# Bias rows stored from 128 partitions in eight parts, and the third FFN's first two units alternated with halves of the compression

## The chip, the cores and the metric

The kernel runs on one core of one Trainium2 chip. The metric is the device time of one execution, in microseconds. A profile is one execution of the program, taken by the hardware profiler; times in it count from the start of its span. The engines are TensorE (PE, with its weight loads as PEld), VectorE (DVE), ScalarE (ACT), GpSimd (POOL) and SyncE (SP), which issues most of the DMAs.

## What is computed

Two transformer blocks run one after the other on x of 1 x 256 x 1024, float32. The first has three attention branches and an MLP of width 4096. The second has four SwiGLU FFNs of width 2816 (FFN 0 to 3 in the kernel), a gated spatial mixer between FFN 0 and 1, and an attention with compressed, selected and window keys between FFN 2 and 3. Two pieces of the second block matter here:

```
def swiglu(x, w1, w3, w2):
    return (jax.nn.silu(x @ w1) * (x @ w3)) @ w2

def compress(kv, pe, w1, b1, w2):      # once for keys, once for values
    ...
    blocks = blocks + pe[None, None, :, None, :]
    flat = blocks.transpose(0, 1, 3, 2, 4).reshape(B, n_cmp, G, CMP_LEN * Dh)   # 15 blocks, 2048 wide
    return jax.nn.gelu(flat @ w1 + b1, approximate=False) @ w2                  # w1: 2048 x 256

    def head_bias(dist):               # rel_table: 32 buckets x 16 heads
        return rel_table[rel_bucket(dist)].reshape(dist.shape + (G, HG)).transpose(2, 3, 0, 1)
```

The bias of a head depends on the distance alone, so one row of 383 numbers for each of the 16 heads holds all of it. The third FFN and the compression are independent of each other: the compression reads what the second FFN left, and is used only in the attention behind the third.

## The kernel before

**Units and the ring.** Every weight comes in units of 128 x 2048 float32 (1 MiB). The order of the units is the list that `plan_units` returns. SyncE loads them in that order into a ring of three slots; a load waits until the unit three places earlier has been split, or, for the compression's units ("cw", i), which aren't split, until TensorE has used it (the semaphore `unit_used`, raised by the first matmul behind a unit: `settle`). Splitting means two float32r halves: ScalarE copies the unit, which rounds it (L1438), VectorE subtracts (L1858), and the two go into one of three split slots; the last unit of a stage goes into the tensor `two`. For ten-odd units GpSimd subtracts in place of VectorE (L2460); ("w3", 0, 0) is one of them. A product of float32 numbers is then three matmuls.

**The stages' order** is written out by hand for each engine, and each engine goes through its own list in order. `plan_tiles` gives every TensorE output a PSUM bank: banks 0 to 3 in turn for tiles, banks 4 to 7 for the accumulators of the down products, which `clear_acc` zeroes before a stage and which the norm behind the stage reads.

**The MLP** has 16 chunks of 256 hidden columns. A chunk is 48 matmuls of the up unit, relu on ScalarE (L1610), square and split on VectorE (L2193, L2174, L2176; the last one raises `hid_ready`), and 48 matmuls of the down unit, done one chunk later. `down_last` at the end does half of the last but one down unit, then alternates with the last, so that the norm can start by halves of rows. The first matmuls of the next FFN follow as soon as the rows' transposes are there.

**The bias rows.** While the MLP's first chunks run, TensorE makes the 16 rows with one matmul (`rel_rows`, 33 x 16, against `onehot`, 33 x 383), VectorE copies them out (L2220), and GpSimd stores each head's row 128 times into the DRAM tensor `rel_scratch`, one DMA for each head (L2504), paced by `hid_ready`. Head h waits for h + 1 hidden chunks, 14 at most. Behind the stores in GpSimd's queue come ("w3", 0, 0), the gain rows and the mixer's constants. The scratch is read back once, skewed, for the attention late in the kernel.

**The third FFN** (f = 2) starts, without a norm of its own, behind the keys' and values' units. TensorE does the keys' compression (two units, 64 columns a matmul, straight from the ring), the unit ("w1", 2, 0), the values' compression, ("w3", 2, 0), the clears, and then chunk by chunk. ScalarE does four gelus of the compression (L1762), rounds ("w3", 2, 0), then ("w1", 2, 1), and goes on with the silus. The values' compression writes to the banks that the keys' compression had.

Of the kernel before, what the change touches and what calls it, by code (L numbers as in the profile page):

```python
# [81 lines left out]
def plan_units():  # L82
# [21 lines left out]
    u += third[0:1] + [("cw", i) for i in range(2, 4)] + third[1:]  # L104
# [30 lines left out]
def plan_tiles():  # L135
# [42 lines left out]
    names += [("ch", s, m) for s in range(2) for m in range(2)]  # L178
    names += ffn(2) + half_norm(7, 0) + [("ck",), ("cv",)] + half_norm(7, 1)
    names += [("qg",)] + [("q", i) for i in range(8)] + [("qt",)]  # L180
    names += mix(MIX2) + norm(8) + ffn(3) + norm(9)
    held, out, turn = [0] * 4, {}, 0
    for seq, name in enumerate(names):
        if name[0] == "m":
            bank = name[1] % MLP_BODY
        elif name[0:2] == ("n", 2):
            bank = 2 + name[3]
        elif name[0] == "hm":
            bank = 3 - name[1]
        elif name[0] == "rel":  # L190
            bank = 3
        elif name[0:2] == ("ch", 1):
            bank = out[("ch", 0, name[2])][0]
        else:
            bank, turn = turn % 4, turn + 1
# [65 lines left out]
WO_EARLY = 2  # L261

# [33 lines left out]
def two_blocks(nc, t, out):  # L296
    ctx = ExitStack()
    with ctx:
# [95 lines left out]
        rel_out = take(at, N_REL)[0:NH]  # L394
# [58 lines left out]
        tile_read = [sem(f"tile_read{i}") for i in range(4)]  # L453
# [7 lines left out]
        rel_out_ready, rel_stored, rel_back = sem("rel_out_ready"), sem("rel_stored"), sem("rel_back")  # L461
# [123 lines left out]
        def _(sp):  # L585
# [135 lines left out]
        def _(pe):  # L721
# [338 lines left out]
            def mlp(n):  # L1060
# [79 lines left out]
            def ffn(f, between=None):  # L1140
# [11 lines left out]
                def first_by_features():  # L1152
# [33 lines left out]
                clear_acc()  # L1186
                done = MLP_CHUNKS + f * FFN_CHUNKS + (8 if f else 0)

                def chunk(c):
# [7 lines left out]
                    up_w3(tiles, parts(("w3", f, c + 1), KT))  # L1197
                    have(("w2", f, c))
# [112 lines left out]
            def compress(s):  # L1311
                tiles = [open_tile(("ch", s, m)) for m in range(2)]
                pe.wait_ge(cx_ready, s + 1)
                for h in range(2):
                    have(("cw", 2 * s + h))
                    for m in range(2):
                        for j in range(8):
                            ins = mm(tiles[m][:, 0:HD], up_unit(("cw", 2 * s + h))[:, j, m * P:(m + 1) * P],
                                     cx[:, s, 8 * h + j].rearrange("p g i -> p (g i)"), h == 0 and j == 0,
                                     h == 1 and j == 7)  # L1320
                            if j == 0:
                                settle(ins)
                        if h:
                            ins.then_inc(tile_done, 1)
                    owed[0] += 1

            compress(0)
            ffn(2, lambda: compress(1))
# [84 lines left out]
        def _(act):  # L1413
# [234 lines left out]
            def ffn(f, following):  # L1648
# [110 lines left out]
            for s in range(2):  # L1759
                for m in range(2):  # L1760
# [61 lines left out]
        def _(dve):  # L1822
# [355 lines left out]
            def mlp():  # L2178
# [34 lines left out]
                by_tokens(0)  # L2213
                low_hidden(0)
# [5 lines left out]
                dve.tensor_copy(rel_out, o[0:NH, 0:N_REL]).then_inc(frees(("rel",)), 1)  # L2220
# [231 lines left out]
        def _(pool):  # L2452
# [56 lines left out]
            pool.wait_ge(rel_stored, 16 * NH)  # L2509
# [75 lines left out]
```

## Time and profile before

| | us |
| --- | --- |
| median of 3 runs | 1580.91 |
| lowest and highest | 1579.22, 1581.44 |
| the profiled execution | 1582.14 |
| its span | 1580.4 |
| TensorE busy in the span | 1507.0 (95%) |
| VectorE busy | 932.0 (59%) |
| ScalarE busy | 658.6 (42%) |
| GpSimd busy | 105.2 (7%) |
| share of TensorE in the chain that ended last | 83% |

The page lists, for the whole span, the busy time of each engine, the chain of work that ended last and the costliest groups of instructions. A matmul's busy time overlaps with the next one's. Behind an instruction in a timeline stands, in brackets, how long its engine was idle before it and what ended that. The mean granted clock of TensorE over the span is 0.97 of full speed.

### The profile page before, as it was taken

What the parts mean: (1) busy time and instruction counts of PE and PEld (TensorE: products, weight loads), DVE (VectorE), ACT (ScalarE), POOL (GpSimd) and SP (SyncE); (2) the same over time, 40 slices, a digit from 0 to 9 for tenths busy, and PEclk for the clock granted to TensorE, in tenths of its full rate; (3) what the DMA queues carried; (4) which work ended last, traced back from release to release, by engine and by line L of the source; (5) the groups of instructions that cost most, each with busy time, mean ns of one, the idle gap of its engine ahead of it and who ended that gap; (6) DMA issues with size and microseconds to landing.
All of it is one profiled execution on the core that took longest, in us unless ns stands there. A gap on an engine that the chain in (4) does not pass through costs nothing.

```text
span 1580.4 us, 25559 instructions
## 1 busy us (share of the span) xinstructions
PE 1507.0 (95%) x10597; PEld 1372.9 (87%) x10608; DVE 932.0 (59%) x1370; ACT 658.6 (42%) x831; POOL 105.2 (7%) x85
## 2 busy tenths in 40 slices
PE   8989999999789999999999999989999999999997
PEld 6978977898679999998889998989999876799997
DVE  5886367565475556657775556635555464365556
ACT  5655433343234334453343334333333455343332
POOL 0012141000020000100010001000001120100000
PEclk9999999999989999999999999999999988999999
DMA  7533445999956556564456555575555510355651
GB/s 251 159 111 105 159 163 138 192 217 208 162 193 230 190 191 211 172 187 160 141 194 194 185 190 191 168 237 190 192 188 177 187 54 1 107 167 189 190 191 64
DMA packets 191639, 268.45 MB, mean 170 GB/s; under 512 B 5852, under 2 KB 164736, under 8 KB 191294
## 3 DMA queue, kind: packets, MB, share of 16 engines
q1 hardware_dynamic: 186336, 250.05, 48.1%
q0 software_dynamic: 4336, 15.91, 7.9%
q10 hardware_dynamic: 878, 1.21, 0.3%
q8 instruction: 66, 1.08, 0.3%
q14 instruction: 23, 0.19, 0.0%
HBM read 261.92 MB, written 4.19 MB: 168 GB/s over the span
## 4 chain that ended last, share of the span: by engine, by line
PE 83%; DVE 8%; DMA 3%; ACT 3%; issue 1%; POOL 0%; SPq 0%; DVEq 0%; ACTq 0%
PE bank L725 81%; PE bank L748 2%; DVE split L1858 2%; ACT split L1438 2%; DMA ring<-in_ffn_w 1%; DMA ring<-in_w_mlp_out 1%; DVE resid L1935 1%; DVE resid L1943 1%; DVE stats L1914 1%; DVE resid L1912 1%; DMA ring<-in_w_in 1%; ACT act_out L1460 0%; DVE hid_hi L2174 0%; DVE arena L2055 0%; ACT gain_rows L1564 0%
## 5 line engine op out<-in xcount | busy, mean ns | idle before, releaser
L725 PE MATMUL bank<-hT_hi,split 128*128 128x256 f32 (+1 forms) x3984 | 717.5, 281 | 10.9 <-ACT act_out L1576 5.4
L1858 DVE TENSOR_TENSOR split<-ring,split 128x2048 fp32r<-128x2048 f32 x210 | 479.6, 2285 | 388.7 <-ACT split L1438 383.5
L725 PEld LDWEIGHTS bank<-hT_hi,split 128*128 128x128 f32 (+1 forms) x3984 | 616.2, 189 | 18.1 <-issue 8.9
L1438 ACT ACTIVATE split<-ring 128x2048 fp32r<-128x2048 f32 (+1 forms) x224 | 426.8, 1907 | 365.2 <-PE bank L725 327.3
L725 PE MATMUL bank<-hT_lo,split 128*128 128x256 f32 (+1 forms) x1992 | 558.4, 280 | 0.0
L725 PEld LDWEIGHTS bank<-hT_lo,split 128*128 128x128 f32 (+1 forms) x1992 | 376.3, 189 | 2.4
L725 PE MATMUL bank<-split,hid_hi 128*128 128x512 f32 x992 | 288.8, 397 | 0.3 <-DVE split L1858 0.2
L725 PEld LDWEIGHTS bank<-split,hid_hi 128*128 128x128 f32 x992 | 182.9, 189 | 41.2 <-issue 1.2
L725 PE MATMUL bank<-split,hT_hi 128*128 128x256 f32 (+1 forms) x896 | 179.0, 298 | 6.7 <-DVE split L1858 4.4
L725 PE MATMUL bank<-split,hid_lo 128*128 128x512 f32 x496 | 160.0, 396 | 0.0
L725 PEld LDWEIGHTS bank<-split,hT_hi 128*128 128x128 f32 x896 | 143.9, 190 | 15.2 <-DVE split L1858 5.1
L2460 POOL TENSOR_TENSOR split<-ring,split 128x2048 fp32r<-128x2048 f32 x14 | 64.2, 4583 | 1034.5 <-ACT split L1438 866.1
L725 PE MATMUL bank<-split,hT_lo 128*128 128x256 f32 (+1 forms) x448 | 129.9, 296 | 0.0
L1610 ACT ACTIVATE act_out<-bank 128x256 f32<-128x256 f32 (+1 forms) x104 | 43.2, 417 | 179.1 <-PE bank L725 179.0
L725 PEld LDWEIGHTS bank<-split,hid_lo 128*128 128x128 f32 x496 | 93.5, 188 | 22.3
L725 PEld LDWEIGHTS bank<-split,hT_lo 128*128 128x128 f32 x448 | 85.3, 190 | 2.4
L725 PE MATMUL bank<-arena 64*128 64x256 f32 (+6 forms) x442 | 70.8, 322 | 12.6 <-DVE row_max L2072 4.5
L725 PEld LDWEIGHTS bank<-arena 64*128 64x128 f32 (+4 forms) x442 | 51.7, 179 | 29.8 <-issue 12.8
L2176 DVE TENSOR_TENSOR hid_lo<-hid,hid_hi 128x256 fp32r<-128x256 f32 (+1 forms) x112 | 51.4, 459 | 4.0 <-DVE hid_hi L2174 0.2
L2271 DVE SCALAR_TENSOR_TENSOR hid<-act_out,bank 128x256 f32<-128x256 f32 x82 | 34.3, 418 | 30.6 <-ACT act_out L1610 30.6
L725 PE MATMUL bank<-two,hid_hi 128*128 128x512 f32 x96 | 34.9, 416 | 18.1 <-DVE hid_lo L2176 18.1
L2174 DVE CAST hid_hi<-hid 128x256 fp32r<-128x256 f32 (+1 forms) x112 | 39.0, 348 | 3.8
(202 smaller groups left out, 994.0 us busy)
## 6 DMA issues: line engine op xcount, KB each, us to landing
ring<-in_ffn_w SPq DMA_DIRECT2D x132, 1024.0 KB, 5.3
ring<-in_w_in SPq DMA_DIRECT2D x19, 1024.0 KB, 5.2
ring<-in_w_mlp_in SPq DMA_DIRECT2D x16, 1024.0 KB, 9.3
ring<-in_w_mlp_out SPq DMA_DIRECT2D x16, 1024.0 KB, 7.9
ring<-in_sgu_w_in SPq DMA_DIRECT2D x16, 1024.0 KB, 5.5
ring<-in_sgu_w_out SPq DMA_DIRECT2D x8, 1024.0 KB, 4.9
ring<-in_kv_w SPq DMA_DIRECT2D x6, 1024.0 KB, 5.4
ring<-in_w_out SPq DMA_DIRECT2D x4, 1024.0 KB, 5.0
```

The lines of the kernel that those rows point to most:

```text
L725: ins = pe.matmul(o, lhsT, rhs, start=start, stop=stop)
L748: return pe.transpose(o, a, ident[0:n, 0:n])
L1438: act.activation(halves(q, n)[0], ring[:, u % SLOTS, 0:n], ACT.Copy).then_inc(hi_ready, 1)
L1610: act.activation(act_out[:, b, 0:cols], banks[b][:, 0:cols], func).then_inc(act_ready, 1)
L1858: dve.tensor_tensor(lo, ring[:, u % SLOTS, 0:n], hi.bitcast(F32), ALU.subtract).then_inc(split_ready, 1)
L1912: link(dve.scalar_tensor_tensor(out=r, in0=r, scalar=ALPHA if n >= 4 else 1.0, in1=acc[2 * b + h][:, :], op0=ALU.mult, op1=ALU.add))
L1914: link(dve.bn_stats(stats[:, b, h, :], r))
L1935: link(dve.scalar_tensor_tensor(out=d, in0=r, scalar=mv[:, b, 0:1], in1=gain_bc[:, cols], op0=ALU.subtract, op1=ALU.mult))
L2174: dve.tensor_copy(hi, raw).then_inc(hid_rounded, 1)
L2176: return dve.tensor_tensor(lo, raw, hi.bitcast(F32), ALU.subtract)
L2271: dve.scalar_tensor_tensor(out=raw, in0=act_out[:, b, 0:S], scalar=0.5, in1=banks[b][:, S:2 * S], op0=ALU.mult, op1=ALU.mult).then_inc(til ...
L2460: pool.tensor_tensor(split_lo[:, place, :], ring[:, u % SLOTS, :], split_hi[:, place, :].bitcast(F32), ALU.subtract).then_inc(split_ready, 1)
```

## The change

The bias rows: `rel_rows` is copied to `rel_wide`, where each head's column stands eight times, so that the matmul gives 128 rows. Each partition then stores its row 16 times, in eight DMAs of two copies from all 128 partitions. Part j waits for j + 3 hidden chunks.

The third FFN: the order of the units becomes ("w1", 2, 0), ("cw", 2), ("w3", 2, 0), ("cw", 3), ("w1", 2, 1) and so on, and TensorE does the values' compression in two halves, one behind each of the first two units. Its output goes to banks 5 and 6, two accumulators, and the clears move behind the second pair of units and behind ScalarE's gelus. ScalarE rounds ("w3", 2, 0) right behind the keys' gelus and does the values' gelus behind the first two silus.

```diff
@@ plan_units
-    u += third[0:1] + [("cw", i) for i in range(2, 4)] + third[1:]
+    u += third[0:1] + [("cw", 2)] + third[1:2] + [("cw", 3)] + third[2:]
@@ plan_tiles
-    names += [("ch", s, m) for s in range(2) for m in range(2)]
-    names += ffn(2) + half_norm(7, 0) + [("ck",), ("cv",)] + half_norm(7, 1)
+    third = ffn(2)
+    names += [("ch", 0, m) for m in range(2)] + third[0:2] + [("ch", 1, m) for m in range(2)] + third[2:]
+    names += half_norm(7, 0) + [("ck",), ("cv",)] + half_norm(7, 1)
...
-            bank = out[("ch", 0, name[2])][0]
+            bank = 5 + name[2]
@@ SyncE, ffn
                 if f == 2:
                     load(("cw", 2))
+                load(("w3", f, 0))
+                if f == 2:
                     load(("cw", 3))
-                load(("w3", f, 0))
@@ TensorE, mlp
                 pe.wait_ge(rel_in, 32)
-                pe.wait_ge(fills, 2)
+                pe.wait_ge(rel_wide_ready, 1)
                 o = open_tile(("rel",))
-                ins = mm(o[0:NH, 0:N_REL], rel_rows, onehot, True, True)
+                ins = mm(o[:, 0:N_REL], rel_wide, onehot, True, True)
@@ TensorE, ffn
-                    between()
+                    between(0)
                     have(("w3", f, 0))
                     up_w3(tiles, parts(("w3", f, 0), KT))
+                    between(1)
...
-                clear_acc()
+                if f in TOK:
+                    clear_acc()
...
+                    if c == 0 and f not in TOK:
+                        for m in range(2):
+                            tile_copied(pe, ("ch", 1, m))
+                        clear_acc()
@@ TensorE, the compression
-            compress(0)
-            ffn(2, lambda: compress(1))
+            pe.wait_ge(cx_ready, 1)
+            compress(0, 0)
+            compress(0, 1)
+
+            def second_compression(h):
+                pe.wait_ge(cx_ready, 2)
+                compress(1, h)
+
+            ffn(2, second_compression)
@@ ScalarE, ffn
                     silu(0, 0)
                     silu(0, 1)
+                    between()
                     rounds(0)
@@ ScalarE, the third FFN
+            compressed(0)
             round_unit(("w3", 2, 0))
-            ffn(2, (("qg", 0), ("q", 0)))
+            ffn(2, (("qg", 0), ("q", 0)), lambda: compressed(1))
@@ VectorE, mlp
                 by_tokens(0)
+                dve.wait_ge(rel_in, 32)
+                dve.wait_ge(fills, 2)
+                dve.tensor_copy(rel_wide.rearrange("p (h r) -> p h r", h=NH),
+                                rel_rows.unsqueeze(2).to_broadcast([33, NH, P // NH])).then_inc(rel_wide_ready, 1)
                 low_hidden(0)
...
-                dve.tensor_copy(rel_out, o[0:NH, 0:N_REL]).then_inc(frees(("rel",)), 1)
+                dve.tensor_copy(rel_out, o[:, 0:N_REL]).then_inc(frees(("rel",)), 1)
@@ GpSimd
-            for h in range(NH):
-                pool.wait_ge(hid_ready, min(h + 1, MLP_CHUNKS - 2))
-                pool.dma_start(rel_dram.ap()[h:h + 1], rel_out[h:h + 1, :].unsqueeze(1).to_broadcast([1, P, N_REL])
-                               ).then_inc(rel_stored, 16)
+            copies = NH // REL_PARTS
+            rows = rel_dram.ap().rearrange("h (r i) n -> (h r) i n", r=P // NH)
+            for j in range(REL_PARTS):
+                pool.wait_ge(hid_ready, j + 3)
+                pool.dma_start(rows[:, j * copies:(j + 1) * copies, :],
+                               rel_out.unsqueeze(1).to_broadcast([P, copies, N_REL])).then_inc(rel_stored, 16)
```

`REL_PARTS` is 8, and the two later waits on `rel_stored` ask for 16 * REL_PARTS in place of 16 * NH.

## Rows read from the trace of the kernel before

**Rows 1.** The list of waits of TensorE: engine, line, waited for; us in total, times, longest.

```profile
PE bank L725 <- DVE hid_lo L2176: 18.3, 2, 18.1
```

**Rows 2.** The timeline of TensorE at the MLP's end: start, us, what.

```profile
409.36 0.27 PE L725 MATMUL bank<-hT_hi,split 128*128 128x256 f32 x1
...
420.56 0.27 PE L725 MATMUL bank<-hT_hi,split 128*128 128x256 f32 x1
...
423.24 0.40 PE L725 MATMUL bank<-split,hid_hi 128*128 128x512 f32 x1
441.76 0.77 PE L725 MATMUL bank<-two,hid_hi 128*128 128x512 f32 x1 [18.13 <-DVE hid_lo L2176]
...
453.31 0.36 PE L725 MATMUL bank<-split,hT_hi 128*128 128x256 f32 x1
```

**Rows 3.** The timelines of the other engines and SP's queue in that stretch.

```profile
401.35 1.55 POOL L2504 DMA_DIRECT2D rel_scratch<-arena  x3 [10.68 <-DVE hid_lo L2176]
...
403.28 0.38 SPq L642 DMA_DIRECT2D ring<-in_w_mlp_out  x1
...
427.33 1.91 ACT L1438 ACTIVATE two<-ring 128x2048 fp32r<-128x2048 f32 x1 [15.25 <-DMA ring<-in_w_mlp_out]
...
411.10 0.43 DVE L2174 CAST hid_hi<-hid 128x512 fp32r<-128x512 f32 x1
411.56 0.69 DVE L2176 TENSOR_TENSOR hid_lo<-hid,hid_hi 128x512 fp32r<-128x512 f32 x1
...
436.24 4.65 DVE L2174 CAST hid_hi<-hid 128x512 fp32r<-128x512 f32 x1
```

**Rows 4.** The DMA issues of the whole run: KB each, median us to landing.

```profile
rel_scratch<-arena POOLq DMA_DIRECT2D x16, 191.5 KB, 9.3
...
out<-resid SPq DMA_DIRECT2D x4, 256.0 KB, 2.0
```

**Rows 5.** The timeline of TensorE at the first FFN's end.

```profile
633.05 0.39 PE L725 MATMUL bank<-two,hid_hi 128*128 128x512 f32 x1
...
643.27 0.36 PE L725 MATMUL bank<-split,hT_hi 128*128 128x256 f32 x1
```

**Rows 6.** The DMA queues between 255 and 445 us: packets, MB, share.

```profile
q1 hardware_dynamic: 21749, 33.54, 49.6%
q0 software_dynamic: 1034, 3.16, 45.4%
```

**Rows 7.** The timeline of TensorE at the third FFN's start.

```profile
1027.83 0.36 PE L725 MATMUL bank<-hT_hi,split 128*128 128x256 f32 x1
...
1033.52 7.25 PE L725 MATMUL bank<-arena,ring 128*128 128x64 f32 x64
...
1045.30 0.58 PE L725 MATMUL bank<-hT_hi,split 128*128 128x256 f32 x1 [4.53 <-DVE split L1858]
...
1053.85 0.47 PE L725 MATMUL bank<-hT_hi,split 128*128 128x256 f32 x1
```

**Rows 8.** The timeline of ScalarE in that stretch.

```profile
1026.31 1.28 ACT L1762 ACT_TABLE_LOAD   x1 [4.96 <-PE bank L725]
1027.61 0.76 ACT L1762 ACTIVATE arena<-bank,colv 128x60 f32<-128x60 f32 x2
...
1041.02 1.90 ACT L1438 ACTIVATE split<-ring 128x2048 fp32r<-128x2048 f32 x1
```

**Rows 9.** SP's queue there, and the second of its two compression loads (1025 to 1028.3).

```profile
1024.70 3.89 SPq L642 DMA_DIRECT2D ring<-in_cmp_w  x2
...
ring<-in_cmp_w SPq DMA_DIRECT2D x1, 1024.0 KB, 5.8
```

**Rows 10.** Three stretches: from:to, length, busy of each engine, granted clock, DMA share, GB/s.

```profile
268.00:269.00 1.00, 0.17 (x2) 0.14 (x2) 0.79 (x2) 1.00 (x1) 0.00 (x0) 1.00 0.89 273
1272.00:1273.00 1.00, 0.24 (x2) 0.00 (x0) 1.00 (x4) 0.15 (x1) 0.55 (x1) 1.00 0.15 57
1275.00:1276.00 1.00, 1.00 (x6) 0.86 (x5) 0.90 (x6) 0.52 (x3) 0.00 (x0) 0.63 1.09 386
```

More of the change, by code:

```diff
@@ L177, in plan_tiles @@
     names += [("kT", s, f) for s in (0, 1, 2, 4) for f in range(2)]
-    names += [("ch", s, m) for s in range(2) for m in range(2)]
-    names += ffn(2) + half_norm(7, 0) + [("ck",), ("cv",)] + half_norm(7, 1)
+    third = ffn(2)
+    names += [("ch", 0, m) for m in range(2)] + third[0:2] + [("ch", 1, m) for m in range(2)] + third[2:]
+    names += half_norm(7, 0) + [("ck",), ("cv",)] + half_norm(7, 1)
     names += [("qg",)] + [("q", i) for i in range(8)] + [("qt",)]
     names += mix(MIX2) + norm(8) + ffn(3) + norm(9)
-    held, out, turn = [0] * 4, {}, 0
+    held, out, turn = [0] * 8, {}, 0
     for seq, name in enumerate(names):
@@ L261 @@
 WO_EARLY = 2
+REL_PARTS = 8
 def rounded_before(f):
@@ L393, in two_blocks @@
         onehot = take(at, N_REL)[0:33]
-        rel_out = take(at, N_REL)[0:NH]
+        rel_out = take(at, N_REL)
+        rel_wide = take(at, P)[0:33]
         at = [2 * KT * S]
@@ L452, in two_blocks @@
         tile_done = sem("tile_done")
-        tile_read = [sem(f"tile_read{i}") for i in range(4)]
+        tile_read = [sem(f"tile_read{i}") for i in range(7)]
         x_in = [sem(f"x_in{b}") for b in range(NB)]
@@ L460, in two_blocks @@
         cw2_in = sem("cw2_in")
-        rel_out_ready, rel_stored, rel_back = sem("rel_out_ready"), sem("rel_stored"), sem("rel_back")
+        rel_wide_ready, rel_stored, rel_back = sem("rel_wide_ready"), sem("rel_stored"), sem("rel_back")
         cols_ready = sem("cols_ready")
@@ L1309, in _, with compress @@
                 owed[0] += 1
[L1311 to L1325, printed above, removed]
-            compress(0)
-            ffn(2, lambda: compress(1))
+            def compress(s, h):
+                tiles = [bank_of(("ch", s, m)) if h else open_tile(("ch", s, m)) for m in range(2)]
+                have(("cw", 2 * s + h))
+                for m in range(2):
+                    for j in range(8):
+                        ins = mm(tiles[m][:, 0:HD], up_unit(("cw", 2 * s + h))[:, j, m * P:(m + 1) * P],
+                                 cx[:, s, 8 * h + j].rearrange("p g i -> p (g i)"), h == 0 and j == 0,
+                                 h == 1 and j == 7)
+                        if j == 0:
+                            settle(ins)
+                    if h:
+                        ins.then_inc(tile_done, 1)
+                owed[0] += 1
+            pe.wait_ge(cx_ready, 1)
[5 more added lines that the diff above has]
+            ffn(2, second_compression)
             pe.wait_ge(cw2_in, 32)
@@ L1646, in mlp, with ffn @@
                 round_unit(("w3", 0, 0))
-            def ffn(f, following):
+            def ffn(f, following, between=None):
                 first = ("w1", f, 1)
@@ L1758, in _, with compressed @@
             act.wait_ge(fills, 4)
-            for s in range(2):
+            def compressed(s):
                 for m in range(2):
@@ L2501, in _ @@
             tile_copied(pool, ("rel",))
-            for h in range(NH):
-                pool.wait_ge(hid_ready, min(h + 1, MLP_CHUNKS - 2))
-                pool.dma_start(rel_dram.ap()[h:h + 1], rel_out[h:h + 1, :].unsqueeze(1).to_broadcast([1, P, N_REL])
-                               ).then_inc(rel_stored, 16)
+            copies = NH // REL_PARTS
[4 more added lines that the diff above has]
+                               rel_out.unsqueeze(1).to_broadcast([P, copies, N_REL])).then_inc(rel_stored, 16)
             low_unit(("w3", 0, 0))
             load_rows(4)
-            pool.wait_ge(rel_stored, 16 * NH)
+            pool.wait_ge(rel_stored, 16 * REL_PARTS)
             pool.dma_start(ws, t["sgu_w_s_2"][0].rearrange("g p s -> p g s")).then_inc(sgu_in, 16)
@@ L2531, in _ @@
             pool.memset(pc, 0.0).then_inc(fills, 1)
-            pool.wait_ge(rel_stored, 16 * NH)
+            pool.wait_ge(rel_stored, 16 * REL_PARTS)
             pool.dma_start(rel, bass.AP(rel_dram, P - 1, [[N_REL - 1, P], [P * N_REL, NH], [1, S]])).then_inc(rel_back, 16)
```

## The prediction

> **What bounds the kernel now.** I read the list of what TensorE waited for first. One entry stands out, a single wait of 18.1 us that ended with VectorE's low half of a hidden chunk [rows 1]. TensorE is busy nearly everywhere else, so the time is its own work plus a few holes, and a change pays only by what it takes out of a hole or adds to one. Then I read TensorE's timeline on both sides of that hole, and the other engines' in the same stretch. The last block of the MLP opens with twelve products of the old chunk (ending about 423.5) and stops; it goes on at 441.76 and reaches the first product of the next FFN at 453.31 [rows 2]. VectorE is the name in the wait, but not the cause. ScalarE rounded the last down unit at 427.33, as soon as it had landed, and everything in its queue came behind it. That unit was issued at 403.28, 24.05 us earlier, and 2 us ahead of it GpSimd had issued the last three row stores [rows 3]. VectorE's cast then sat 4.65 us at 436.24, where it takes 0.43 us in the loop, because GpSimd's own subtraction of ("w3", 0, 0) ran at the same time [rows 3]. So three things in a row: stores, then a late load, then a collision. The second hole is in the third FFN: 4.53 us ahead of its first w3 unit, after which the matmuls run at half the clock for a while [rows 7].
>
> **Why the stores hurt.** A store of 191.5 KB takes 9.3 us to land, about 21 GB/s; a store of 256 KB from 128 partitions takes 2.0 us, 128 GB/s, at the end of the kernel [rows 4]. Between 255 and 445 us the GpSimd queue moved 3.16 MB in 45.4% of the sixteen engines' time, the weights 33.54 MB in 49.6% [rows 6]: nearly nine times as much time for each byte. What differs is that each old store reads one partition (one head's row, repeated 128 times).
>
> **Part 1, the stores.** The same 3.1 MB now go out in 8 parts of 383 KB, from 128 partitions (each head's row on eight). Added: one VectorE copy of 33 x 128 after the first by_tokens, a bias matmul that makes 128 rows where it made 16 with the same 383 columns, and a copy of 128 x 383 where it was 16 x 383. The last two have the length of their free size, so nothing; the first is bounded by 0 and about half a microsecond (the cast of 128 x 512 in the loop is 0.43) and falls where VectorE waits for TensorE and ScalarE anyway, so I take 0. The wait on rel_wide_ready stands ahead of a matmul that comes a whole down block later. GpSimd's stores now wait for hidden chunks 3 to 10 instead of 1 to 14; behind them in its queue are only ("w3", 0, 0) and the gain rows, both needed after 415 us. A chunk takes 11.20 us (409.36 to 420.56, rows 2), so the last part, four chunks ahead of the stores of 401.35, goes out at about 356.5, some 47 us before the load that was late. No row shows a GpSimd store from 128 partitions. From below its price is the 2.0 us of the output store scaled by size, 3 us; from above it is the old time for each byte, 5.4 us of all sixteen engines for an old store, so 10.8 for a part. I take the former, since partitions are the only thing that changed. The Trainium skill (SBUF — State Buffer, "Door 1: the DMA port swizzle") gives 27.6 GB/s for partitions 0 to 3 and 328 for all 128, both for 1 MiB; the old stores' 21 GB/s agrees, and by it a part would take some 3 us as well.
>
> Now what is late next. The load of 403.28 lands by 410 (5.8 us without such stores beside it, rows 9) and the next three follow as slots come free. In the loop the low half of a hidden chunk ends at 412.25, 2.6 us after the last up product of its chunk (409.36 and 0.27); one chunk of 11.20 later that is 423.45 [rows 2, 3]. TensorE's twelve products of cover end at 423.47, so it starts the last unit at about 423.7: a hole of 0.3 us instead of 18.1. The collision goes too: ScalarE rounds ("w3", 0, 0) only after the last relu, so GpSimd starts near 423.3, after the cast. From the first product of the last unit to the first of the next FFN the same code takes 10.22 us at full clock in the first FFN (633.05 to 643.27) and took 11.55 here [rows 2, 5]. So 453.31 becomes 423.7 + 10.2 = 433.9, a gain of 19.4 us; the RMS norm here has shorter VectorE steps than the layer norm of the twin, worth up to 0.6 more. I take **19.5 us**.
>
> **Part 2, the third FFN.** Before, from 1033.52: the second compression 7.25 us, the hole 4.53 us (ScalarE in its order does both gelus of that compression before it rounds w3, at 1041.02), then w3 and the clears until 1053.85, 8.55 us, where a unit at full clock takes 5.7 (1027.83 to 1033.52) and the clears some 0.7 [rows 7, 8]. So 4.5 + 2.2 = 6.7 us can be had.
>
> After, in order. A half of the compression is 3.6 us. The w3 load takes the place of ("cw", 3), the second issue in the row of 1024.70, at 1028.2, and lands as that one did after 5.8 us, at 1034.0 [rows 9]. From ScalarE's rounding to TensorE's first product is 4.28 us (1041.02 to 1045.30, rows 7, 8): w3 can start at 1038.3, where TensorE is free at 1033.5 + 3.6 = 1037.1, a hole of 1.2. ("w1", 2, 1) now takes the ring slot of ("cw", 2), which is freed by the first product behind it, at 1038.7; it lands at 1044.5 and can be used at 1048.8. TensorE is free at 1038.3 + 5.7 + 3.6 = 1047.6: a hole of 1.2 again. ScalarE goes on from 1046.5 with a table load, two silus, another table load and two gelus (1.28 + 0.8 + 1.28 + 0.8, rows 8) and rounds ("w3", 2, 1) at 1050.6, usable at 1054.9; TensorE wants it at 1048.8 + 5.7 = 1054.5: 0.4. The moved clears cost what they did. Behind the new wait of ScalarE for the second compression are three roundings, of which only that one is near. The sum: 6.7 - 1.2 - 1.2 - 0.4 = **3.9 us**. The new banks 5 and 6 remove a wait that was already met, so nothing.
>
> **Does a hole of 1.2 us cost clock?** A wait of 0.83 us at 268 left the granted clock at 1.00; one of 1.05 us in 1272 to 1273, in a stretch of small matmuls, was followed by 0.63 in 1275 to 1276 [rows 10]. The stretch here is dense like that of 268, so I take no fall; one fall would cost the 2.2 us above.
>
> **Sum.** 19.5 + 3.9 = 23.4 us. The profiled execution took 1582.14 us with a span of 1580.4, the median of the three runs is 1580.91; the difference of 1.2 us is kept out, and the gain is taken from the median: 1557.5 us (1558.7 against the profiled execution).
>
> **Rivals.**
> (a) Part 2 gives little or nothing. Its holes cost clock once or twice (2.2 each), or the loads come a microsecond later. For it: three new waits within 20 us; against it: TensorE is dense between them. Time 1580.9 - 19.5 less 2 or 0 = 1559.4 to 1561.4.
> (a2) A switch of ScalarE's tables costs twice its load. The change puts two switches ahead of the third rounding; at 1.28 us more for each, the third hole is 3.0 us instead of 0.4 and the clock falls behind it (2.2), so part 2 comes out at 3.9 - 2.6 - 2.2 = -0.9 and the time at 1562.3. Against it: the load of 1026.31 takes 1.28 us and the gelu stands right behind it at 1027.61 [rows 8]. The Trainium skill (ScalarE: Activation LUTs, "What ACT_TABLE_LOAD costs") has it this way, with a drain of about 1.38 us beside each load.
> (b) The collision stays. If ("w1", 0, 0), issued at about 408.4, lands later than some 417, VectorE is late for the last cast and meets GpSimd: 4.6 us and a fall of clock of 2.2, so 1564. Loads without such stores beside them land in 5.8, so this needs 3 us more.
> (c) Slower. The time of a store is a price for each byte, not for reading one partition. Then a part holds the sixteen engines 10.8 us, two weight units 5.9 (94 us for 33.54 MB, rows 6), together 16.7 us in a chunk of 11.20: eight chunks would each be 5.5 us longer, 44 us, against 23 gained: 1602. It begins to hurt where a part costs over 5.3 us, and eats the gain from 8.2. Against it: the 2.0 us of the output store.
> (d) The change doesn't do what it says: another late load keeps the hole near 18 us, and only part 2 shows: 1577.
>
> **How the numbers follow.** Forecast 0.74, (a) 0.11, (a2) 0.03, (b) 0.05, (c) 0.05, (d) 0.02. The low end is part 2 without any hole and the 0.6 of the norm: 1580.9 - 20.1 - 6.7 = 1554.1, taken as 1553.5 for the offset of single runs; the high end takes in (a) and (a2), 1562.5. Left out are (b), (c), (d). This kernel can be told from no change at about 0.2% (3 us). Forecast, (a), (a2) and (b) are faster by more, 0.93, and half of (d) with them, 0.94; same is the other half, 0.01; slower is (c), 0.05.
>
> **What would show it.** Part 1: the 18.1 us wait gone from TensorE's list, stores landing in about 3 us, weight units in the MLP landing near 6, the cast back at 0.43, next FFN 19 to 20 us earlier. Part 2: three waits of about 1 us instead of 4.5, granted clock 1.00 throughout, two more table loads. I am wrong if the stores take over 5 us each, or if the new waits are longer than 2 us and the clock falls.

## The result, and the profile after

The changed kernel takes 1557.13 us (median of 4 runs, 1551.82 to 1560.56), against 1580.98 for the kernel before on the same chip (4 runs, 1579.22 to 1581.44): a ratio of 0.985, with an interval of 0.981 to 0.988. That is 23.9 us less; forecast were 23.4. The profiled execution took 1553.93 us, with a span of 1552.2 and a granted clock of 0.98.

**Part 1.** First the list of what TensorE waited for: engine, line, waited for; us in total, times, longest.

```profile
PE bank L729 <- ACT act_out L1591: 8.9, 3, 3.9
PE bank L729 <- DVE split L1877: 5.4, 4, 3.7
...
PE bank L752 <- DMA shared_rows<-in_cmp_pe: 4.4, 1, 4.4
```

The entry of 18.1 us [rows 1] is gone, and the longest that are left are waits of 4.4, 3.9 and 3.7 us elsewhere. TensorE's timeline at the MLP's end (start, us, what) answers to [rows 2]:

```profile
419.57 0.27 PE L729 MATMUL bank<-hT_hi,split 128*128 128x256 f32 x1
...
422.25 0.40 PE L729 MATMUL bank<-split,hid_hi 128*128 128x512 f32 x1
422.60 0.47 PE L729 MATMUL bank<-two,hid_hi 128*128 128x512 f32 x1
...
432.30 0.35 PE L729 MATMUL bank<-split,hT_hi 128*128 128x256 f32 x1
```

The last unit, the one in `two`, now follows the twelve products of cover without a wait. The next FFN starts at 432.30, where it was 453.31. The MLP's last chunk was 0.99 us earlier anyway (419.57 against 420.56), so 20.0 us are gained here. The timelines of the other engines and of SP's queue in that stretch, as [rows 3]:

```profile
355.49 0.72 POOL L2529 DMA_DIRECT2D rel_scratch<-arena  x1 [10.48 <-DVE hid_lo L2195]
422.38 4.63 POOL L2483 TENSOR_TENSOR split<-ring,split 128x2048 fp32r<-128x2048 f32 x1 [66.17 <-ACT split L1453]
...
402.29 0.38 SPq L645 DMA_DIRECT2D ring<-in_w_mlp_out  x1
...
410.98 1.91 ACT L1453 ACTIVATE two<-ring 128x2048 fp32r<-128x2048 f32 x1
...
421.30 0.43 DVE L2193 CAST hid_hi<-hid 128x512 fp32r<-128x512 f32 x1
```

All three links of the old chain are broken. The last store goes out at 355.49. The load of 402.29 is rounded at 410.98 with no wait for a DMA in brackets, so it landed in less than 8.7 us, where it took 24. The cast takes 0.43 us and ends before GpSimd's subtraction starts at 422.38. In the kernel before the two ran side by side: this is GpSimd's row there, beside the cast of 4.65 us at 436.24 [rows 3].

```profile
436.12 4.49 POOL L2460 TENSOR_TENSOR split<-ring,split 128x2048 fp32r<-128x2048 f32 x1 [33.22 <-ACT split L1438]
```

The DMA queues between 255 and 445 us (packets, MB, share of the sixteen engines' time) and three of the groups of issues there (KB each, median us to landing) answer to [rows 4] and [rows 6]:

```profile
q1 hardware_dynamic: 21760, 33.56, 56.8%
q0 software_dynamic: 1349, 4.89, 7.7%
...
ring<-in_w_mlp_out SPq DMA_DIRECT2D x14, 1024.0 KB, 5.0
ring<-in_w_mlp_in SPq DMA_DIRECT2D x13, 1024.0 KB, 6.0
...
rel_scratch<-arena POOLq DMA_DIRECT2D x8, 383.0 KB, 6.0
```

GpSimd's queue moved half as much again as in [rows 6] (gain rows and the mixer's constants fall into the stretch now) and took 7.7% of the engines' time where it took 45.4%.

**Part 2.** TensorE's timeline at the start of the third FFN, as [rows 7]:

```profile
1006.57 0.36 PE L729 MATMUL bank<-hT_hi,split 128*128 128x256 f32 x1
...
1012.26 3.68 PE L729 MATMUL bank<-arena,ring 128*128 128x64 f32 x32
1016.48 0.39 PE L729 MATMUL bank<-hT_hi,split 128*128 128x256 f32 x1 [0.54 <-DVE split L1877]
...
1022.19 3.68 PE L729 MATMUL bank<-arena,ring 128*128 128x64 f32 x32
1026.31 0.38 PE L729 MATMUL bank<-hT_hi,split 128*128 128x256 f32 x1 [0.44 <-DVE split L1877]
```

One wait of 4.53 us has become two of 0.54 and 0.44, with a half of the values' compression ahead of each. The granted clock is 1.00 in every stretch of 10 us from 1005 to 1045.

**The run stage by stage.** A stage is taken from the first residual add of one norm to that of the next, by VectorE's timeline (before: 235.28, 444.70, 634.64, 787.33, 977.42, 1220.94, 1376.17, 1565.3 us; after: 234.61, 424.27, 613.66, 766.02, 956.15, 1194.09, 1347.98, 1537.1). Each row is one profiled execution; the kernels with a name are the experiments below. The stages behind the MLP that aren't shown (the first, second and last FFN and the mixer) differ by at most 1.0 us. What lies ahead of the MLP isn't touched by any of these edits either, but it took 230.9 us (e5) to 238.1 us (e3).

| us | MLP | keys, values and third FFN | attention |
| --- | --- | --- | --- |
| before | 209.4 | 243.5 | 155.2 |
| after | 189.7 | 237.9 | 153.9 |
| e1 stores only | 189.8 | 243.4 | 151.5 |
| e2 compression only | 209.0 | 238.5 | 157.2 |
| e3 one partition, early | 201.7 | 238.5 | 153.8 |
| e4 wide, late | 189.6 | 238.4 | 157.1 |
| e5 pairs 32 apart | 231.6 | 238.5 | 153.8 |
| e6 single last store | 208.5 | 243.6 | 159.9 |
| e7 filled | 189.0 | 238.4 | 149.8 |
| e8 after, again | 189.2 | 238.8 | 165.7 |
| e9 other order | 202.1 | 243.4 | 155.2 |
| e10 filled more | 189.2 | 238.4 | 149.6 |

So the first part is worth 19.3 to 20.2 us (19.7 from before to after) and the second 4.6 to 5.6, by any pair of rows that differ in one of them. The attention, which the change doesn't touch, runs from 149.6 to 165.7 us, the widest spread of any stage. It is looked at in e7, e8 and e10; the spread of 7.2 us ahead of the MLP was not.

### The profile page after: what moved, and what is told of

It reads as the page before. It is cut to its first block, busy times and chain, and to the rows that moved or that the text cites. A ratio compares the mean times of both kernels' runs of the same rounds, so it can differ in the third digit from the quotient of the medians.

```text
span 1552.2 us, 25559 instructions
## 1 busy us (share of the span) xinstructions
PE 1499.2 (97%) x10597; PEld 1367.3 (88%) x10608; DVE 927.9 (60%) x1371; ACT 660.7 (43%) x833; POOL 102.7 (7%) x77
## 4 chain that ended last, share of the span: by engine, by line
PE 86%; DVE 8%; ACT 3%; issue 1%; DMA 1%; POOL 0%; DVEq 0%; ACTq 0%
PE bank L729 84%; PE bank L752 2%; DVE split L1877 2%; ACT split L1453 1%; DVE resid L1954 1%; DVE resid L1962 1%; DVE stats L1933 1%; DVE resid L1931 1%; DMA ring<-in_ffn_w 1%; ACT act_out L1475 0%; DVE stats L1891 0%; DVE arena L2074 0%; ACT gain_rows L1579 0%; DMA resid<-in_x 0%; ACT arena L1524 0%
## 5 line engine op out<-in xcount | busy, mean ns | idle before, releaser
L2193 DVE CAST hid_hi<-hid 128x256 fp32r<-128x256 f32 (+1 forms) x112 | 34.8, 311 | 3.8
L729 PE MATMUL bank<-act_out,arena 128*64 128x128 f32 x296 | 36.9, 286 | 0.0
```

The source lines that it names most:

```text
L729: ins = pe.matmul(o, lhsT, rhs, start=start, stop=stop)
L2193: dve.tensor_copy(hi, raw).then_inc(hid_rounded, 1)
```

## The experiments

**e1 and e2: each part alone.** e1 is the kernel before with the diff's `rel_wide`, its copy and the eight stores; e2 is the kernel before with all the rest of the diff.

> The kernel before with the stores' part of the change alone. Theory (the two parts add up, the stores are worth about 20 us): about 1560.5 us, the 18.1 us wait gone from TensorE's list, the 4.5 us wait ahead of the third FFN's w3 unit still there with the half clock behind it. Rival (the gains overlap, or a quicker MLP shifts loads so that the third FFN's wait changes): not additive, under 1557 or over 1565.

> The kernel before with the third FFN's part alone. Theory: 1575 us (6 us less than before, as the profile of the changed kernel has it at the third FFN; my sum on record was 3.9, which would give 1577), the 18.1 us wait unchanged, and two waits of about 0.5 us in the third FFN at full clock. Rival (this part is worth nothing by itself, since a slower state of the clock takes it back): 1580 to 1581.

e1 took 1559.93 us, a ratio of 0.987 (0.985 to 0.989). Its MLP is 189.8 us long, the 18.1 us wait is gone, and the 4.5 us wait of the third FFN is back. e2 took 1578.33 us, 0.997 (0.996 to 0.999); its MLP is 209.0, with a wait of 17.7 us. The two medians are 21.4 and 3.0 us under the 1581.36 of the kernel before beside them, together 24.5, against 23.9 for the whole change: the parts add up. e1 is where it was expected. e2 gave 3.0 us (1.4 to 6.6 by the interval) where about 6 were expected. Its stage is 5.0 us shorter; in its profiled execution the attention was 2.0 and the part ahead of the MLP 2.2 us longer than in that of the kernel before.

**e3: is it the width of the stores, or their place?** The changed kernel, with stores from one partition at the eight early points, two at each, from partitions 8h and 8h + 8.

```diff
-                pool.dma_start(rows[:, j * copies:(j + 1) * copies, :],
-                               rel_out.unsqueeze(1).to_broadcast([P, copies, N_REL])).then_inc(rel_stored, 16)
+                for h in (2 * j, 2 * j + 1):
+                    pool.dma_start(rel_dram.ap()[h:h + 1], rel_out[8 * h:8 * h + 1, :].unsqueeze(1)
+                                   .to_broadcast([1, P, N_REL])).then_inc(rel_stored, 16)
```

> The changed kernel, but each head's row is stored from one partition again, two stores of 191.5 KB in place of each part of 383 KB, at the same eight points. Theory (reading one partition is what costs): the stores land in 9 us or more each, the two take 10.8 us of the DMA engines in a chunk of 11.2 beside 5.9 for the weights, so the weights come late all through these chunks: up to 44 us more than the changed kernel, 1590 to 1601 us. Rival (what the change gained came only from not storing near the MLP's end): the same as the changed kernel, 1557, with weights that still land in time.

It took 1567.36 us, 0.991 (0.989 to 0.993), better than the 1590 to 1601 that I had expected if width is all. The queues between 270 and 430 us, the landings of the sixteen stores, and two groups of loads between 270 and 375 us, while the stores run:

```profile
q1 hardware_dynamic: 17123, 27.46, 50.2%
q0 software_dynamic: 1024, 3.14, 30.6%
...
DMA to landing us min/median/max: 8.4/10.3/13.9
...
ring<-in_w_mlp_out SPq DMA_DIRECT2D x8, 1024.0 KB, 16.1
ring<-in_w_mlp_in SPq DMA_DIRECT2D x8, 1024.0 KB, 15.0
```

30.6% of 160 us for 16 stores is 3.1 us of all sixteen engines for a store, not the 5.4 of the kernel before. The direction was right: while the stores run, the weight units take 15 to 16 us to land in the median, and the MLP is 12.0 us longer than after. The size was wrong by three to four times. So something besides the number of partitions sets the price. Besides the early place, two things differ from the kernel before: all stores go out in pairs, and the two of a pair come from partitions 8 apart.

**e4: the place alone.** The eight wide stores, held back to the points of the old ones: part j waits for j + 7 hidden chunks.

```diff
-                pool.wait_ge(hid_ready, j + 3)
+                pool.wait_ge(hid_ready, j + 7)
```

> The changed kernel, but part j waits for hidden chunk j + 7 in place of j + 3, so that the last part goes out where the last old stores did, 2 us ahead of the last down unit's load. Theory (width is what counts): that load lands in 6 to 10 us instead of 24, there is no wait over 1 us at the MLP's end, and the time is the changed kernel's, 1557 within 3 us. Rival (any store there delays the last down unit): a wait of several us at the end of the MLP and the half clock behind it, 1565 or more.

It took 1557.28 us (0.985, 0.983 to 0.987), with an MLP of 189.6. The last store goes out at 400.47, just ahead of the last down unit's load, as the last three did before [rows 3], and no wait follows. The early place is worth nothing. But e4 keeps two things of the change, the width and that no stores go out in a burst, and it doesn't say whether both are needed. The old stores that went out alone did no harm that shows. These are the two of the kernel before ahead of its last burst at 401.35:

```profile
378.88 0.52 POOL L2504 DMA_DIRECT2D rel_scratch<-arena  x1 [10.68 <-DVE hid_lo L2176]
390.15 0.52 POOL L2504 DMA_DIRECT2D rel_scratch<-arena  x1 [10.75 <-DVE hid_lo L2176]
```

They are one chunk of 11.2 to 11.3 us apart, and a chunk is no longer than that after the change. Sixteen stores from one partition, each by itself, were not tried.

**e5: two stores from partitions 32 apart.** As e3, but paired so that the two partitions of a point lie 32 apart; the number, the size and the points of the stores are those of e3.

```diff
-                for h in (2 * j, 2 * j + 1):
+                for h in (j + 4 * (j // 4), j + 4 * (j // 4) + 4):
```

> As e3 (one partition for each store, two stores of 191.5 KB at each of the eight points), but the two stores of a point read partitions 32 apart (heads h and h + 4, partitions 8h and 8h + 32) in place of partitions 8 apart. In e3 the sixteen stores took 38.6% of 127 us of the sixteen DMA engines, 3.1 us each, where the kernel before had 5.4 each, and the MLP's stretch was 12 us longer than the changed kernel's. Theory (what a store costs is a shared way out of SBUF: two partitions with the same way queue, two with different ways don't): the pair takes 18 to 20 us to land, 5.4 us of engine time for each store, and the MLP is some 30 to 44 us longer than the changed kernel's: 1587 to 1601 us. Rival (the way doesn't matter, each partition has its own rate): as e3, 1567 us.

It took 1596.77 us, 1.010 (1.008 to 1.012), as expected: slower than the kernel before, and 29.4 us above e3 in the medians (29.9 in the MLP's stage), for the same sixteen stores, two at each of the same points. The queues between 270 and 430 us, with the landings of the stores:

```profile
q0 software_dynamic: 1024, 3.14, 49.1%
q1 hardware_dynamic: 13392, 22.02, 38.3%
...
ring<-in_w_mlp_in SPq DMA_DIRECT2D x11, 1024.0 KB, 17.0
ring<-in_w_mlp_out SPq DMA_DIRECT2D x10, 1024.0 KB, 17.0
...
DMA to landing us min/median/max: 9.4/15.1/19.7
```

49.1% of 160 us is 4.9 us a store. A pair takes 9.8 us of the sixteen engines here and 6.1 in e3; one store alone took 5.4 in the kernel before. Two stores from partitions 8 apart take little more of the engines' time than one, though they overlap only in part: in the kernel before a store that goes out alone lands in 8.8 to 9.5 us (from 303.71 on), and here the later one of a pair in 11.3 to 13.9 (e3). From partitions 32 apart (e5) the later one takes 15.8 to 19.7 us, and the pair's price is nearly that of two single stores. That they share a way out is what the Trainium skill (SBUF — State Buffer, "Door 1: the DMA port swizzle") states: a partition 32 further on is on the same port, and a port serves eight partitions. With 5.9 us for the two weight units of a chunk [rows 6], a chunk needs 15.7 us of the DMA engines here and 12.0 in e3, where TensorE needs 11.20: eight times the excess is 36 and 6 us, and the MLP was 41.9 and 12.0 us longer than after; the 6 us that are missing in each are not explained. The pairs of e5 also lie four heads apart in DRAM, where those of e3 are neighbours. That speaks against the DRAM side as the cause only together with e9 below, where the stores of the last burst lie four heads apart too, and that burst is faster than one of neighbours. This is the mechanism of rival (c), and nearly its price of 44 us, from the stores that the change did away with.

**e6: without the three stores that go out together at the end.** The kernel before, with the waits of the stores moved forward by two chunks, so that none is left over for a last burst.

```diff
-                pool.wait_ge(hid_ready, min(h + 1, MLP_CHUNKS - 2))
+                pool.wait_ge(hid_ready, max(h - 1, 1))
```

> The kernel before, with its sixteen stores of one partition each, but head h waits for h - 1 hidden chunks (at least 1) in place of h + 1 (at most 14): three stores go out at the first point and one at the last, where before it was two and three. Theory (the hole of 18 us comes from three stores in one burst just ahead of the last down unit's load): that load lands in 9 to 14 us, in time, the 18.1 us wait is gone, the MLP's stretch is 190 to 192 us in place of 209.4, and the time 1562 us. Rival (any store of one partition there makes the last unit late): a wait of 5 us or more stays, 1570 or more.

It took 1583.76 us, 0.999 (0.997 to 1.002): no gain, where 1562 was expected. The late wait did go: the last down unit, issued at 424.32, was rounded at 434.26. But the waits' floor put four stores together at the start (I had counted on three), and the timelines of GpSimd, ScalarE and TensorE show what followed:

```profile
272.46 2.11 POOL L2504 DMA_DIRECT2D rel_scratch<-arena  x4 [17.04 <-DVE arena L2220]
...
311.41 1.91 ACT L1438 ACTIVATE split<-ring 128x2048 fp32r<-128x2048 f32 x1 [22.12 <-DMA ring<-in_w_mlp_out]
...
315.77 1.21 PE L725 MATMUL bank<-split,hid_hi 128*128 128x512 f32 x2 [15.92 <-DVE split L1858]
```

ScalarE waited 22.1 us for a unit of `w_mlp_out`, TensorE 15.9 us for the split halves that come from it, and the MLP is 208.5 us long. The hole has only moved. It belongs to a burst of stores, wherever it stands, not to the place at the end of the MLP, and TensorE doesn't wait when a single store from one partition goes out just ahead of the last load.

**e9: the same three stores at the end, from other partitions.** The kernel before; heads 0, 4, 8, 12, 1, 5, and so on, so that the last three come from partitions 7, 11 and 15 in place of 13, 14 and 15.

```diff
-                pool.dma_start(rel_dram.ap()[h:h + 1], rel_out[h:h + 1, :].unsqueeze(1).to_broadcast([1, P, N_REL])
+                g = 4 * (h % 4) + h // 4
+                pool.dma_start(rel_dram.ap()[g:g + 1], rel_out[g:g + 1, :].unsqueeze(1).to_broadcast([1, P, N_REL])
```

> The kernel before; only the order of the sixteen one-partition stores is changed: heads 0, 4, 8, 12, 1, 5, 9, 13, 2, ... instead of 0, 1, 2, ... The last three, which go out together late in the MLP, are then those of partitions 7, 11 and 15 in place of 13, 14 and 15, so they lie in three different groups of four partitions. Nothing else moves, and every store is still alone or in its burst of three at the same point. Theory (partitions of one group of four share one way out, so a burst from one group holds the weights up longest): the load of the last down unit lands some 12 us after its issue instead of 24, TensorE's wait there shrinks from 18 us to 2 to 6 us, and the time is 1565 to 1570. Rival 1 (a burst of three one-partition stores costs the same from anywhere): wait of 18 us stays, 1580 to 1583. Rival 2 (only pairs 32 apart share a way, so nothing was shared before either and nothing changes): as rival 1.

It took 1575.72 us, 0.995 (0.993 to 0.997), 8.0 us under the kernel before beside it, without one instruction more or less. That is faster than either rival allows and slower than I had expected. The timelines of GpSimd, SP's queue, ScalarE, VectorE and TensorE:

```profile
403.96 1.55 POOL L2505 DMA_DIRECT2D rel_scratch<-arena  x3 [10.68 <-DVE hid_lo L2176]
430.82 4.49 POOL L2460 TENSOR_TENSOR split<-ring,split 128x2048 fp32r<-128x2048 f32 x1 [25.30 <-ACT split L1438]
...
405.89 0.38 SPq L642 DMA_DIRECT2D ring<-in_w_mlp_out  x1
...
423.21 1.92 ACT L1438 ACTIVATE two<-ring 128x2048 fp32r<-128x2048 f32 x1 [8.52 <-DMA ring<-in_w_mlp_out]
...
430.93 4.66 DVE L2174 CAST hid_hi<-hid 128x512 fp32r<-128x512 f32 x1
...
436.46 0.77 PE L725 MATMUL bank<-two,hid_hi 128*128 128x512 f32 x1 [10.21 <-DVE hid_lo L2176]
```

The landings of the sixteen stores, first in the kernel before, then in e9; the longest is in both the third store of the last burst:

```profile
DMA to landing us min/median/max: 8.8/9.3/22.8
...
DMA to landing us min/median/max: 8.8/9.0/16.1
```

The unit landed 17.3 us after its issue, not 24.0, and the wait is 10.2 us in place of 18.1. Spreading three stores over three groups of partitions gives back 6.7 us of the load, not the 12 expected. The third store lands 6.7 us sooner after its issue, and the load 2.1 us behind it in both kernels (425.21 and 427.31 before, 421.08 and 423.19 here): the three stores overlap only in part, as the pairs of e3 do, and the load still ends behind them. And the collision of the old chain stays whole: the cast took 4.66 us beside GpSimd's subtraction. That alone is 4.2 of the 10.2 us. So the third link of the chain has a price of its own (the 4.6 of rival (b)), and it came with both late loads, of 24.0 and 17.3 us.

**e7, e8 and e10: the attention.** TensorE's timeline in the changed kernel's attention has three such waits between small matmuls, here the first and the last (the other is of 1.92 us at 1252.21):

```profile
1246.48 3.81 PE L729 MATMUL bank<-arena 64*128 64x256 f32 x16 [1.09 <-DVE row_max L2091]
...
1309.13 0.65 PE L729 MATMUL bank<-arena 32*64 32x128 f32 x2 [3.52 <-ACT act_out L1591]
```

Right behind the first, and at the end of the third, the granted clock falls to half. In e7 and e10 products of zeros, which nobody reads, are put ahead of these waits; the output is the same. e7 has 8 and 14 of them ahead of two score pairs and 24 ahead of the third wait, e10 has 18, 28 and 24. e8 is the changed kernel once more, for the comparison on the same chip as e7.

```diff
+            def fill(n, bank=o_bank):
+                nil = zeros[:, :].bitcast(BF16)
+                for _ in range(n):
+                    settle(mm(bank[:, S:2 * S], nil[:, 0:P], nil[:, 0:S], True, True))
...
                 for p in range(4):
+                    if n < 6 and p == 3:
+                        fill(8 if n == 4 else 14)
                     score_pair(n, p)
...
+                        if (n, p) == (N_BATCH - 3, 1):
+                            fill(24, open_tile(("T", n, 2)))
                         values(n, p - 1)
```

> The changed kernel with idle matmuls of zeros (46 of 256 columns, into parts of banks that nobody reads) ahead of three waits of TensorE in the late attention: 8 ahead of one of 1.1 us, 14 ahead of one of 1.9 us, 24 ahead of one of 3.5 us. Between the six profiles so far this stretch took 151.5 to 157.2 us, and the granted clock was at half for different lengths behind these waits. Theory (the clock falls behind these waits and is what makes runs of one kernel differ): the granted clock stays at 1.00 there, the stretch takes 142 to 147 us, the time is 1545 to 1551 us, and the runs lie closer together. Rival (the fillers come too late or delay what waits, or the small matmuls there let the clock fall anyway): 1554 to 1560.

> The changed kernel as it is, beside e7 on the same chip. Both theories: 1552 to 1561 us.

> The changed kernel with idle products of zeros ahead of attention waits as in e7_filled, but 18 and 28 of them in place of 8 and 14 ahead of the last score pair of batches 4 and 5, because waits of 0.8 and 1.3 us were left there at 1255 and 1260 us and the granted clock stood at half from 1262 to 1270. Output unchanged. Theory (a wait of one to two us between small matmuls is what the clock falls behind): no fall in the attention, time lost at half clock under 1 us where e7_filled had 3.4, time 1548 to 1551, against 1552.6 for e7_filled. Rival (the clock falls from time to time whatever is filled, or because the small matmuls themselves are too light): still 3 us or more at half clock, 1552 to 1555.

e7 took 1552.59 us (0.981, 0.979 to 0.983), e8 1565.67 (0.989, 0.986 to 0.993), e10 1550.46 (0.979, 0.978 to 0.980). e8 missed its 1552 to 1561: the same program that had measured 1557.13 is 8.5 us slower in this later run. e7 is 13.1 us faster than e8 beside it, and no run of the one reaches the other. e10, which ran apart from both, has the lowest median of this study: 0.979 of the kernel before, where the changed one is at 0.985 and, as e8, at 0.989. Two stretches of e8, in the columns of [rows 10]; the granted clock is the third number from the end:

```profile
1310.00:1330.00 20.00, 20.00 (x79) 13.72 (x78) 1.51 (x6) 3.33 (x7) 0.00 (x0) 0.50 0.00 1
1330.00:1350.00 20.00, 18.66 (x70) 13.07 (x70) 5.34 (x4) 6.32 (x8) 0.00 (x0) 0.59 0.10 30
```

One of e7, where its clock falls once more:

```profile
1262.00:1270.00 8.00, 8.00 (x44) 6.77 (x44) 6.15 (x37) 5.35 (x20) 0.00 (x0) 0.68 0.00 0
```

The same stretch of e10, and one behind the wait at 1309:

```profile
1262.00:1270.00 8.00, 7.13 (x50) 4.97 (x49) 6.24 (x35) 4.06 (x18) 0.00 (x0) 1.00 0.00 0
1308.00:1326.00 18.00, 17.43 (x118) 12.05 (x118) 3.16 (x13) 6.29 (x14) 0.00 (x0) 1.00 0.00 1
```

And TensorE's timeline in e10, just ahead of the first of the two:

```profile
1259.01 1.13 PE L729 MATMUL bank<-arena 64*128 64x256 f32 x4 [1.30 <-DVE row_max L2100]
```

For each stretch of 2 us of the attention take its length by one minus the granted clock. The sum, the shortfall of the clock, is 13.7 us before, 11.9 after, 22.2 in e8, 3.4 in e7 and none in e10. The attention's length goes with it, but not one for one: the profile after has 11.9 us more of it than e10 and is only 4.3 longer, probably because idle products take time too and a slow clock costs nothing where TensorE waits. e8 stood at half clock for some 37 us behind a wait of 3.52 us at 1309.03, the same wait as at 1309.13 in the changed kernel's first profile, where the clock was back after about 6. The other stages of these two executions differ by under 1 us, the attention by 11.8. e7 missed its 1545 to 1551, and its attention of 149.8 us the 142 to 147. One fall was left in it, behind waits of 0.8 and 1.3 us at 1255 and 1260; e10 filled these further, and the fall went. But its attention still takes 149.6 us, so the fall isn't what e7 missed by: the gain had been set too high. e10's 1550.46 lies in its range of 1548 to 1551, but not for the reason given: its profiled execution is 2.9 us shorter than e7's, and 3.1 us of that lie ahead of the MLP, where the two programs are the same. That filling the large waits shortens the attention is shown by e7 beside e8; that the rest is worth anything is not. And the wait of 1.30 us shown last is still there and no fall follows it, so the length of a single wait doesn't decide it; what does was not found out.

## Why the prediction was right, and where it was off

- **The chain behind the 18.1 us** (stores, then a late load, then a collision): right. e1 takes all of it away by the stores alone, e9 shows the middle and the last link separately.
- **Where the last unit would start.** Forecast 423.7, less the 1 us that all was earlier: 422.7, with a hole of 0.3 behind the cover. Measured 422.60 and no hole. From there to the next FFN 10.2 us were taken from the twin, with up to 0.6 less; measured 9.7. Part 1 was 19.5 in the forecast, and 19.7 in the stages.
- **The price of a wide store: mis-sized in its landing, right in what counts.** I took 3 us from the output's store [rows 4]. They took 6.0 in the median to land (4.8 in e1, 4.9 in e4). Three things differ from that row: they go through GpSimd's queue, each partition writes the same bytes twice, and the weights' stream is beside them; none was tried alone. But what they take from the others is 8.1% of the sixteen engines' time between 270 and 375 us, 8.5 us for eight parts, 1.1 each, where the bound from above was 10.8. I had said "wrong if the stores take over 5 us each": the mark was on the wrong quantity, since nobody waits for their landing.
- **"Partitions are the only thing that changed": right, but not the whole reason.** The old price of 5.4 us a store was not a fixed one for a store from one partition. It is 3.1 in pairs 8 apart (e3), 4.9 in pairs 32 apart (e5). What one way out carries can be estimated from the last burst before, three stores of 191.5 KB from partitions 13 to 15: 23.9 us from the first issue (401.35) to the last landing (425.21), some 25 GB/s. The 21 GB/s of a single old store [rows 4] are near it. So are the 27.6 GB/s that the Trainium skill (SBUF — State Buffer, "Door 1: the DMA port swizzle") gives for partitions 0 to 3.
- **"Nearly nine times as much time for each byte"** was worked out wrong: 45.4% for 3.16 MB against 49.6% for 33.54 MB is 9.7 times. Nothing in the sum rests on it.
- **The early place of the stores**, to which the forecast gave a margin of 47 us, was not needed (e4).
- **Part 2** came out at 5.6 us in this pair of profiles (at 5.0 and 4.7 with e2's 238.5 and e8's 238.8), and at 3.0 in e2's median, where 3.9 were forecast; the sum had three holes of 1.2, 1.2 and 0.4, 2.8 in all, and the trace has 0.54 and 0.44. The steps were right and one size was off. The w3 load was issued 0.39 us after the first w1 product, as forecast (0.37). From rounding to TensorE's first product it was 4.29 us both times (forecast 4.28). But the loads landed in 5.2 and 5.1 us and not 5.8, the time of a compression load that had stood second in a row [rows 9]: 0.6 and 0.7 less, which is the whole difference in the first two holes.
- **The third hole and rival (a2).** ScalarE's timeline, as [rows 8]:

```profile
1022.02 1.91 ACT L1453 ACTIVATE split<-ring 128x2048 fp32r<-128x2048 f32 x1 [7.92 <-DMA ring<-in_ffn_w]
1023.95 1.28 ACT L1625 ACT_TABLE_LOAD   x1
1025.25 0.66 ACT L1625 ACTIVATE act_out<-bank 128x256 f32<-128x256 f32 x2
1025.92 1.28 ACT L1779 ACT_TABLE_LOAD   x1
1027.22 0.51 ACT L1779 ACTIVATE arena<-bank,colv 128x60 f32<-128x60 f32 x2
1027.62 1.91 ACT L1453 ACTIVATE split<-ring 128x2048 fp32r<-128x2048 f32 x1
```

  Two silus took 0.66 us and two gelus 0.51, where I had 0.8 each, and each table load took 1.28 us with the next activation 0.02 us behind it. So ("w3", 2, 1) was rounded in time, and there is no third hole. The drain of 1.38 us that the Trainium skill (ScalarE: Activation LUTs, "What ACT_TABLE_LOAD costs") adds to each load is not to be seen in these rows: the load of 1023.95 starts 0.02 us after the rounding ahead of it ends.
- **No fall of the clock** at the new waits: right, 1.00 from 1005 to 1045.
- **The rivals.** (a) did not come: the new waits are of 0.54 and 0.44 us, and no clock was lost. (b) did not come, since the unit landed in under 8.7 us; e9 shows that its 4.2 us were real. (c) did not come for wide stores; e5 has its mechanism. (d) did not come.
- **The median.** 1557.5 were forecast and 1557.13 measured. That it is so close is luck; that both parts gave about what their sums said is not. The four runs lie between 1551.82 and 1560.56. In the profiles' stages part 2 gave 0.7 to 1.7 us more than forecast, and the attention, for which I had no term, differs by up to 16 us between executions and can hide that, as can the 7 us ahead of the MLP. The same kernel as e8 measured 1565.67, outside the forecast range of 1553.5 to 1562.5, a gain of 16.5 us over the 1582.15 beside it. The next forecast for this kernel needs that spread in its range.

## What to carry to other kernels

When a load is late, look at what else the DMA engines are doing, and ask for each transfer how many partitions its SBUF side spans and which ones: a small store from one partition can keep all sixteen engines busy five times as long as a wide one of twice its size. If a store can't be wide, send one at a time; what must go out together, spread over partitions that don't share a way, and keep it away from loads that are just in time. To count what a transfer costs its neighbours, use its queue's share of the engines' time, not its time to landing.

## What the runs showed of the hardware

- The order of sixteen identical stores alone is worth 8.0 us (e9), and the choice of partitions for stores in pairs 29.4 us (e3 against e5, 29.9 in the MLP's stage). A store from one partition that goes out alone, once in a chunk of 11.2 us, showed no price in TensorE's time.
- The granted clock in the attention is not the same from run to run for the same program: its shortfall was 11.9 and 22.2 us in two executions of the changed kernel, 0 in e10 with idle products in the waits. Filling cost less than it gave: with it the attention took 149.6 and 149.8 us, without it 151.5 to 165.7.
- An engine's busy time is not a measure of what it moves: before, the two queues together held the DMA engines for 95% of the time between 255 and 445 us [rows 6] to move 36.7 MB; after, for 64.5% to move 38.5 MB.
